# Lag matrices of a state-space scan on four column groups of TensorE, and a pair of transposes between two z units

## The reference

```
h = rmsnorm(x, norm_g)
u_a, z_a, u_b, z_b, q, z_x, g_a, g_b, g_x = split(h @ w_in)
# A: 32 groups of 16 channels, 64 complex states each
lam_bar = exp(lam * dt)
bu = einsum('blgh,gph->blgp', u_a, b_bar)
x_t = lam_bar * x_{t-1} + bu_t              # along the 512 rows
y_a = real(einsum('blgp,ghp->blgh', x, c)) + d * u_a
o_a = (glu(gelu(y_a)) * silu(z_a)) @ w_br_ssm
# B: conv of 31 taps over u_b, layernorm, silu, gate z_b, w_br_conv
# X: softmax(q k^T / sqrt(128)) v over 256 tokens, gate z_x, w_br_xatt
x = x + (sigmoid(g_a) * o_a + sigmoid(g_b) * o_b + sigmoid(g_x) * o_x) @ w_out
```

## Time and profile before

| | |
|---|---|
| median of 3 runs | 1183.03 us (1182.65 to 1184.36) |
| profiled execution, its time | 1183.88 us |
| profiled execution, its span | 1182.1 us |
| mean granted TensorE clock (share of full speed) | 0.965 |
| TensorE busy | 1104.3 us, 93% of the span |
| VectorE busy | 812.3 us, 69% |
| GpSimd busy | 468.2 us, 40% |
| ScalarE busy | 425.1 us, 36% |

### The profile page before, as it was taken

The page is one execution under the profiler, slowest core; times in us unless marked ns, Lnnn a source line. Parts: engine busy times, 40 slices in busy tenths (PEclk is TensorE's granted clock), DMA queues, the critical chain, the costliest instruction groups (busy, mean ns, idle before and its releaser), DMA issues.

```text
span 1182.1 us, 20442 instructions
## 1 busy us (share of the span) xinstructions
PE 1104.3 (93%) x8266; PEld 1034.4 (88%) x8266; DVE 812.3 (69%) x1209; ACT 425.1 (36%) x718; POOL 468.2 (40%) x329
## 2 busy tenths in 40 slices
PE   4999998999899999999989899989989999999995
PEld 3749997989899999999956899878989999999994
DVE  4868899797947685344489889988794848744412
ACT  4612543234353442222333245313444445222222
POOL 1027545364223314444312845537332332444440
PEclk9899999899899999999999899989998999999998
DMA  8265314964217733444534342378631484244422
GB/s 213 82 196 155 118 51 118 265 173 124 90 46 139 187 117 122 129 126 139 164 107 139 118 147 73 108 231 189 133 108 46 112 188 134 81 134 136 146 89 73
DMA packets 225300, 155.01 MB, mean 131 GB/s; under 512 B 48690, under 2 KB 201706, under 8 KB 223142
## 3 DMA queue, kind: packets, MB, share of 16 engines
q1 hardware_dynamic: 220454, 144.14, 44.1%
q10 hardware_dynamic: 4752, 9.57, 2.3%
HBM read 130.38 MB, written 24.24 MB: 131 GB/s over the span
## 4 chain that ended last, share of the span: by engine, by line
PE 64%; DVE 19%; POOL 3%; SPq 3%; ACT 3%; DMA 2%; issue 2%; DVEq 0%; ACTq 0%
PE acc L711 41%; PE mp L1046 12%; POOL w_lo L603 3%; DVE cacc L1446 3%; PE mp L752 3%; DVE X L1440 2%; DVE s L1440 2%; PE mp L953 2%; SPq L456 2%; PE mp L652 1%; DVE wt L1440 1%; PE acc L1027 1%; PE mp L923 1%; DVE V L1440 1%; PE mp L814 1%
## 5 line engine op out<-in xcount | busy, mean ns | idle before, releaser
L603 POOL TENSOR_TENSOR w_lo<-w_st,w_hi 128x512 fp32r<-128x512 f32 x288 | 448.0, 1562 | 611.8 <-ACT w_hi L1132 611.2
L1132 ACT CAST w_hi<-w_st 128x512 fp32r<-128x512 f32 x288 | 177.5, 620 | 565.5 <-PE acc L711 390.9
L711 PE MATMUL acc<-h_hi,w_hi 128*128 128x260 f32 x1600 | 333.2, 290 | 7.7 <-POOL w_lo L603 7.7
L711 PE MATMUL acc<-h_lo,w_hi 128*128 128x260 f32 x1600 | 325.4, 285 | 0.0
L711 PE MATMUL acc<-h_hi,w_lo 128*128 128x260 f32 x1600 | 325.2, 285 | 0.0
L711 PEld LDWEIGHTS acc<-h_hi,w_hi 128*128 128x128 f32 x1600 | 251.4, 192 | 16.0 <-issue 15.2
L711 PEld LDWEIGHTS acc<-h_hi,w_lo 128*128 128x128 f32 x1600 | 250.6, 191 | 0.0
L711 PEld LDWEIGHTS acc<-h_lo,w_hi 128*128 128x128 f32 x1600 | 250.0, 191 | 0.0
L1446 DVE SCALAR_TENSOR_TENSOR cacc<-vx,cw,cacc 128x512 f32<-128x512 f32 x232 | 187.0, 879 | 1.8
L1046 PE MATMUL mp<-br_hi,w_hi 128*128 128x260 f32 x384 | 78.6, 286 | 4.3 <-POOL w_lo L603 4.3
L1046 PE MATMUL mp<-br_hi,w_lo 128*128 128x260 f32 x384 | 78.6, 287 | 0.0
(11 more groups left out here) (301 smaller groups left out, 1465.6 us busy)
## 6 DMA issues: line engine op xcount, KB each, us to landing
w_st<-in_w_in SPq DMA_DIRECT2D x208, 256.0 KB, 3.2
g_scratch<-xT ACTq DMA_DIRECT2D x32, 260.0 KB, 2.6
xT<-g_scratch SPq DMA_DIRECT2D x8, 1040.0 KB, 5.6
kb<-in_cache_mem_k SPq DMA_DIRECT2D x16, 512.0 KB, 4.1
kb<-in_cache_mem_v SPq DMA_DIRECT2D x16, 512.0 KB, 4.8
w_st<-in_w_out SPq DMA_DIRECT2D x32, 256.0 KB, 2.8
x_scratch<-xT SPq DMA_DIRECT2D x2, 2080.0 KB, 10.3
xT<-x_scratch SPq DMA_DIRECT2D x4, 1040.0 KB, 5.7
```

The lines of the kernel that those rows point to most:

```text
L603: pool.tensor_tensor(w_lo[:, slot, :], w_st[:, slot, :], w_hi[:, slot, :].bitcast(F32), ALU.subtract).then_inc(w_staged_free, 1)
L711: last = pe.matmul(acc_ps[pair][:, a, 0:HC], w[:, slot, kk * P:(kk + 1) * P], x[:, k, a, :], start=(k == 0 and p == 0), stop=(k == KT - 1 ...
L1132: act.copy(w_hi[:, c % SLOTS, :], w_st[:, c % SLOTS, :]).then_inc(w_hi_done, 1)
```

## The change

The lag matrices of four pairs j are made side by side: the matmul of pair r = 4 g + j goes to columns 32 j to 32 j + 31 of the array (`tile_position`) and to PSUM partitions 32 j to 32 j + 31, at 128 columns for each g. The order is g, ri, j. The output is 128 x 256 in one bank in place of 32 x 1024 in two, and with it `kt`, the skip term's tiles (`eye`, `dcol`, `drow`, `dt`) and the store to DRAM take the form of 128 partitions; the DRAM contents and the reloads of `Mt` stay. The transposes of `ps` go from behind x0's second unit to between its two units on TensorE, and the copy of `psT` from behind both x0 evictions to between them on ScalarE.

```diff
-        eye2 = sb("eye2", [2 * H, H])
+        eye = sb("eye", [P, H])
-        dcol = sb("dcol", [2 * H, Q])
+        dcol = sb("dcol", [P, 4])
-        drow = ur("drow", 1024, [Q, 2 * H])
+        drow = ur("drow", 1024, [4, P])
-        dt = rr("dt", 13072, [2 * H, QH * H])
+        dt = rr("dt", 13072, [P, 2 * H])
-        kt = at(wd_at, 0, 24 * P, "kt", [2 * H, QH, T * H])
+        kt = at(wd_at, 0, 24 * P, "kt", [P, 2, T * H])
...
-                sp.dma_start(drow[:, :], ssm_d[l].rearrange("(q x) -> q x", x=2 * H)).then_inc(sm["p_in"], 16)
+                sp.dma_start(drow[:, :], ssm_d[l].rearrange("(q x) -> q x", x=P)).then_inc(sm["p_in"], 16)
...
                 def toeplitz(half):
...
-                    sp.dma_start(kh.rearrange("(q e) h x -> (e h) q x", e=2), kt[:, :, :]).then_inc(sm["k_out"], 16)
+                    sp.dma_start(kh.rearrange("(r y) h x -> (y h) r x", r=2), kt[:, :, :]).then_inc(sm["k_out"], 16)
...
-                last = transpose(mp[0:2 * H, 2, 256:256 + Q], drow[:, :], Q)
+                last = transpose(mp[:, 2, 256:260], drow[:, :], 4)
...
-                pair("x0")
+                one("x0", 0)
                 wait(pe, l, "ps_norm", 1)
                 pe.sem_inc(entered, 1)
                 for m in range(2):
                     last = transpose(mp[:, 3, m * 32:(m + 1) * 32], ps[:, m * P:(m + 1) * P], 32)
                 last.then_inc(sm["psT_tr"], 1)
+                one("x0", 1)
...
-                    for r in range(QH):
+                    for g in range(2):
                         for ri in range(2):
-                            last = pe.matmul(mp[0:2 * H, r // 4, (r % 4) * P:(r % 4 + 1) * P],
-                                             bd[:, ri, f * QH + r, :, :].rearrange("p e h -> p (e h)"),
-                                             V[:, ri, r, 0:T, :].rearrange("p t h -> p (t h)"),
-                                             start=(ri == 0), stop=(ri == 1))
+                            for j in range(4):
+                                r = 4 * g + j
+                                last = pe.matmul(mp[32 * j:32 * j + 32, 0, g * P:(g + 1) * P],
+                                                 bd[:, ri, f * QH + r, :, :].rearrange("p e h -> p (e h)"),
+                                                 V[:, ri, r, 0:T, :].rearrange("p t h -> p (t h)"),
+                                                 start=(ri == 0), stop=(ri == 1), tile_position=(0, 32 * j))
...
                 one("x0", 0, to_z(2))
-                one("x0", 1, to_z(2))
                 wait(act, l, "psT_tr", 1)
                 wait(act, l, "psT_clear", 1)
                 act.copy(psT[:, :, :, 0:16], mp[:, 3, 0:64].rearrange("p (m g c) -> p m g c", m=2, g=2)).then_inc(sm["psT_ev"], 1)
+                one("x0", 1, to_z(2))
...
-                dve.tensor_copy(dcol[:, :], mp[0:2 * H, 2, 256:256 + Q]).then_inc(sm["par_ev"], 1)
+                dve.tensor_copy(dcol[:, :], mp[:, 2, 256:260]).then_inc(sm["par_ev"], 1)
...
-            tt(eye2[:, :], ident[0:2 * H, 0:H], ident[0:2 * H, H:2 * H], ALU.add)
+            run(dve.tensor_reduce(eye[:, :], ident[:, :].rearrange("p (b h) -> p h b", h=H), op=ALU.add, axis=AX.X))
...
-                    run(dve.tensor_copy(kt[:, :, :].rearrange("h q x -> h (q x)"), mp[0:2 * H, 0:2, :].rearrange("h b x -> h (b x)")))
+                    run(dve.tensor_copy(kt[:, :, :].rearrange("h q x -> h (q x)"), mp[:, 0, 0:2 * P]))
                     dve.sem_inc(sm["k_free"], 1)
                     ta = dt[:, :].rearrange("h (q x) -> h q x", x=H)
-                    tt(ta, eye2[:, :].unsqueeze(1).to_broadcast([2 * H, QH, H]),
-                       dcol[:, f * QH:(f + 1) * QH].unsqueeze(2).to_broadcast([2 * H, QH, H]), ALU.mult)
+                    tt(ta, eye[:, :].unsqueeze(1).to_broadcast([P, 2, H]),
+                       dcol[:, 2 * f:2 * f + 2].unsqueeze(2).to_broadcast([P, 2, H]), ALU.mult)
                     tt(kt[:, :, 0:H], kt[:, :, 0:H], ta, ALU.add)
```

## The result

| | before | after |
|---|---|---|
| median | 1183.78 us (6 runs, 1182.65 to 1185.27) | 1189.49 us (6 runs, 1186.31 to 1192.03) |
| ratio of after to before | | 1.0049, 95% interval 1.0034 to 1.0063 |
| profiled execution, its span | 1183.88 us, 1182.1 us | 1189.94 us, 1188.1 us |
| mean granted clock | 0.965 | 0.962 |

The account below looks back on a forecast made before the run. TensorE was busy 93% of the span, but the last-ending chain lay on it for only 64%. First calls 0, clock +3.6, second calls -1.8 gave +1.8: 1185.7 us profiled, 1184.8 us as median, range 1180.2 to 1189.5.

Parts of the forecast that it names:

- The call's price: Lag matrices on four column groups: a call takes about 1.0 us instead of 3.6, giving TensorE 2.6 us back.
- The first call: Wait for w_lo at x1: gain 0, pause grows from 1.2 to 3.8 us, lower clock costs 1.8 us per layer.
- The second call: Ahead of the second line 953, set by VectorE's scan: gain 0.9 us per layer, with a new 1.7 us TensorE wait.
- The likeliest case: The forecast itself, 1184.8 us, chance 0.42, with a 1.7 us wait ahead of the second line 953.
- Rival 1: New cold start ahead of the second line 953, priced 3.7 us in one layer: 1188.5 us, chance 0.27.
- The move: Transposes of ps and psT's copy placed earlier around x0's units: costs nothing, no wait for psT.
- Rivals 2 to 5: Clock holds at x1, 1181.2 (0.12); whole 2.6 us arrives, 1181.4 (0.12); rival 4; column groups do not overlap, 1183.0 (0.04).
- rival 4: GpSimd gets between VectorE's instructions, x1's pause vanishes, 3.8 us gained per layer: 1173.6 us, chance 0.03.

Follow-up runs that it names:

- the kernel with both calls padded: Changed kernel with matmuls of both lag-matrix calls per layer repeated (7 half calls in place of 2), holding TensorE about as long as before: 1184.09 us, ratio 1.0010.
- the kernel with the second call alone padded: Changed kernel with only each layer's second lag-matrix call repeated, 7 half calls in place of 2: 1183.77 us, ratio 0.9993 to the kernel before.
- the second profile: The changed kernel run again with no edit: 1190.96 us, ratio 1.0060 to the kernel before.
- the stop: Changed kernel with VectorE waiting once in its convolution run for GpSimd's subtractions: 1190.05 us; two instructions later and with the second call padded, 1178.65 us.

## Why the prediction was wrong

- **The call's price** was right: 1.0 us forecast, 1.08 measured. The rule on weight loads that spoke against it, from the Trainium skill's "TensorE: Matmul & The Clock Gate", section "Part 3: Packing small matmuls — row/col tiling", shows no cost in the trace: 34 ns a record, with a load for each, is 3.4 times the old rate.
- **The first call** was right: pauses of 3.65 and 3.66 us (3.8 forecast), ends unmoved, clock low behind them, 1.5 us lost per layer (1.8 forecast; its own rows give 13.28 - 11.54 = 1.74). What it calls the z unit's second half at 254.69 is x1's second unit.
- **The second call** was right in kind: lag copy 0.42 us (0.4), scan's last copy ends at 371.87 where it ended at 372.32, and a pause of 1.7 us ahead of line 956 (1.7). The second stretch gained 1.7 and 1.4 us; in the kernel with both calls padded, where TensorE gains nothing, it still is 0.5 to 1.1 us under before, which leaves 0.6 to 0.9 us for the shorter call (0.9). Against the kernel with the second call alone padded it is 0.1 and 0.8 us, so the size is borne out only roughly.
- **The step that failed** is the price of that last pause. The likeliest case gave it no cost. It came as forecast (1.73 and 1.68 us) and cost 3.3 us in layer 1, and 3.5 and 4.6 us in the two layers of the second profile; with the second call padded, the pause and the loss are gone. Rival 1 named the mechanism, with a chance of 0.27, but had it decide "if the pause passes about 2 us" and held against it that "1.2 us pauses cost nothing", which was read at x1, behind and ahead of products of 260 columns. Also its price was one layer's, 3.7 us; where the clock falls, the third stretch is 3.3 to 5.5 us longer in each layer. The wait of 2.6 us at 402.99 us in the profiled execution had no term either, and why its weights came late is open. That the median, 1189.49 us, lies just within the range, 1189.5, is luck: the same kernel again had 1190.96.
- **What the pauses show together.** "Held" means a granted clock of 1.00 over the next 10 us, in all profiles here. Between line 949 and the second line 956, blocks of 72 columns, pauses of 1.31 to 1.85 us lowered the clock at 11 of 12 places; at x1, pauses of 1.05 to 1.49 us held at 9 of 9. Short products alone do not decide: behind a z unit and ahead of line 949, 1.21 us lowered the clock once and 0.93, 1.05 and 1.29 us held; between transposes of 128 columns (line 652, at 385.23 us in the kernel before, once in every layer), 1.43 us held at 36 of 36. Nor does one reading tell: the pause of 2.2 us ahead of line 1046, from which the prediction took its price, held at 8 of 31 places, and that of 2.7 us ahead of line 760, its row against, at 10 of 18. What decides is not settled by these runs.
- **The move** was right: 1183.05 us alone, and 4.1 us of waiting without it.
- **Rivals 2 to 5** did not come; the stop showed that GpSimd gets in, as rival 4 had it, once VectorE is made to pause, but not for rival 4's price.

What would be forecast with the measured price: 2 x 1.5 - 2 x 0.8 + 2 x 3.3 = +8.0 us, with the lowest price of the clock in both layers; measured are +5.7 and, in the second comparison, +7.1, with executions in which it holds in one. This is an estimate from the rows above.

## What to carry to other kernels

Before shortening a block on the busiest engine, find what its next block waits for; if that is another engine, the saving turns into idle time, and on TensorE idle time has a second price in the clock behind it. Take that price from pauses at the place itself or among like work, in more than one profile, not from one pause of about the same duration. Where such a pause can't be removed, work that may be repeated without harm fills it: here 7 us of repeated products made the kernel before 8.6 and 10.5 us faster in two comparisons, while removing 10 us of real work made it 6 us slower.

## What the runs showed that was not expected

- A pause of 1.21 us ahead of line 949, and one of 0.93 us between its block and line 956, were followed by clocks of 0.62 and 0.66 over 10 us, while pauses of 1.44 to 1.49 us at x1 were followed by 1.00, and 2.61 us at 402.99 as well.
- The same pause costs by chance: behind 1.7 us the clock averaged 1.00, 0.66, 0.66 and 0.51 over 10 us in four places of two profiles of one kernel. It fits that single executions of it lie between 1184.18 and 1193.37 us.
- One stop of VectorE for 2.5 us brought the first line 956 of layer 0 forward by 2.35 us (316.13 to 313.78 us, both with the second call padded).
